# A transformer stack in fp32 pairs: the finished layer norm as operand from the seventh chunk of two feed-forwards on

## The reference

```python
x = layer_norm(ALPHA * x + y, ln_mix_g[layer], ln_mix_b[layer])
x = layer_norm(ALPHA * x + swiglu(x, ffn_w_gate[layer], ffn_w_up[layer], ffn_w_down[layer]),
               ln_ffn_g[layer], ln_ffn_b[layer])

def layer_norm(x, g, b):
    xf = x.astype(jnp.float32)
    mu = xf.mean(-1, keepdims=True)
    var = jnp.mean(jnp.square(xf - mu), -1, keepdims=True)
    return ((xf - mu) * lax.rsqrt(var + LN_EPS) * g.astype(jnp.float32) + b.astype(jnp.float32)).astype(x.dtype)

def swiglu(x, w_gate, w_up, w_down):
    return (jax.nn.silu(x @ w_gate) * (x @ w_up)) @ w_down
```

## Time and profile before

| | |
|---|---|
| median of three runs | 894.04 us (893.62 to 894.8) |
| the profiled execution | 892.68 us |
| its span | 890.9 us |
| TensorE busy | 881.3 us, 99% of the span |
| VectorE, ScalarE, GpSimd busy | 671.4, 511.8, 131.2 us |
| DMA | 156.82 MB |

### The profile page before, as it was taken

How to read it: one execution, slowest core, us unless ns; L and a number is a source line. 1 busy time by engine, 2 the same in 40 slices (tenths; PEclk the granted TensorE clock), 3 DMA queues, 4 the chain that set the end, 5 groups by cost and what they waited for, 6 DMA issues and landing times.

```text
span 890.9 us, 18060 instructions
## 1 busy us (share of the span) xinstructions
PE 881.3 (99%) x6704; PEld 831.8 (93%) x6704; DVE 671.4 (75%) x1114; ACT 511.8 (57%) x763; POOL 131.2 (15%) x89
## 2 busy tenths in 40 slices
PE   9999999999999999999999999999999999999997
PEld 8977999999999999999999999999899999999996
DVE  6976887777777966889766676789877886667666
ACT  7265644434344755977555655567488756555552
POOL 1000000000000043002232240210130122324003
PEclk9999999999999999999999999999999999999999
DMA  8963275555555554435655545434334465565541
GB/s 319 353 223 100 103 246 175 180 205 172 189 191 165 185 189 171 142 120 187 210 176 182 188 169 201 148 133 153 119 119 143 152 226 187 169 198 176 188 142 48
DMA packets 44291, 156.82 MB, mean 176 GB/s; under 512 B 5098, under 2 KB 5589, under 8 KB 44117
## 3 DMA queue, kind: packets, MB, share of 16 engines
q1 hardware_dynamic: 42889, 152.32, 50.2%
q10 hardware_dynamic: 908, 2.28, 0.8%
q0 software_dynamic: 448, 1.59, 0.5%
HBM read 155.11 MB, written 1.06 MB: 175 GB/s over the span
## 4 chain that ended last, share of the span: by engine, by line
PE 89%; DVE 6%; ACT 2%; DMA 1%; issue 1%; POOL 0%; DVEq 0%; POOLq 0%; SPq 0%
PE ps L434 21%; PE ps L435 20%; PE ps L436 20%; PE ps L506 5%; PE ps L508 5%; PE ps L507 5%; DVE w_lo L1476 2%; DMA raw<-in_stream 1%; PE ps L442 1%; PE ps L483 1%; PE ps L477 1%; PE ps L476 1%; PE ps L917 1%; PE ps L620 1%; PE ps L728 1%
## 5 line engine op out<-in xcount | busy, mean ns | idle before, releaser
L434 PE MATMUL ps<-op_hi,w_hi 128*128 128x258 f32 (+1 forms) x1306 | 370.1, 283 | 0.4 <-DVE op_lo L1663 0.4
L435 PE MATMUL ps<-op_lo,w_hi 128*128 128x258 f32 (+1 forms) x1306 | 368.1, 282 | 0.0
L436 PE MATMUL ps<-op_hi,w_lo 128*128 128x258 f32 (+1 forms) x1306 | 367.8, 282 | 0.0
L1476 DVE TENSOR_TENSOR w_lo<-raw,w_hi 128x1024 fp32r<-128x1024 f32 x222 | 283.1, 1301 | 24.7 <-ACT w_hi L1090 22.2
L1090 ACT ACTIVATE w_hi<-raw 128x1024 fp32r<-128x1024 f32 x223 | 230.4, 1052 | 68.8 <-PE ps L436 30.7
L434 PEld LDWEIGHTS ps<-op_hi,w_hi 128*128 128x128 f32 x1306 | 246.2, 188 | 3.8 <-issue 1.8
L435 PEld LDWEIGHTS ps<-op_lo,w_hi 128*128 128x128 f32 x1306 | 246.7, 189 | 1.7
L436 PEld LDWEIGHTS ps<-op_hi,w_lo 128*128 128x128 f32 x1306 | 246.3, 189 | 0.0
L1083 ACT ACTIVATE w_hi<-raw 128x1024 fp32r<-128x1024 f32 x60 | 63.5, 1058 | 60.0 <-PE ps L436 30.2
L434 PE MATMUL ps<-mix_hi,w_hi 128*128 128x256 f32 x336 | 95.6, 284 | 0.0
L436 PE MATMUL ps<-mix_hi,w_lo 128*128 128x256 f32 x336 | 94.1, 280 | 0.0
(11 more groups left out here) (313 smaller groups left out, 1113.8 us busy)
## 6 DMA issues: line engine op xcount, KB each, us to landing
raw<-in_stream SPq DMA_DIRECT2D x283, 512.0 KB, 3.7
bias<-bias_rows POOLq DMA_DIRECT2D x1, 1024.0 KB, 10.8
work<-in_last_norm SPq DMA_DIRECT2D x1, 1024.0 KB, 5.7
result<-y SPq DMA_DIRECT2D x4, 256.0 KB, 2.0
x<-in_x SPq DMA_DIRECT2D x3, 256.0 KB, 5.4
y<-in_spans ACTq DMA_DIRECT2D x1, 640.0 KB
raw<-in_stream SPq DMA_DIRECT2D x2, 256.0 KB, 3.4
bias<-bias_rows POOLq DMA_DIRECT2D x1, 512.0 KB, 13.5
```

The lines of the kernel that those rows point to most:

```text
L434: pe.matmul(o, wh, xh, start=start, stop=False, **kw)
L435: pe.matmul(o, wh, xl, start=False, stop=False, **kw)
L436: return pe.matmul(o, wl, xh, start=False, stop=stop, **kw)
L1476: m = dve.tensor_tensor(w_lo[:, s, :], raw[:, s, :], fp(w_hi[:, s, :]), ALU.subtract)
```

## The change

In the second and third feed-forward the operand of the up units changes at the seventh chunk (chunk 6). From there on it is the finished layer norm as a pair, with 256 columns: chunks 0 to 5 of it in `mix` chunks 2 to 7, chunks 6 and 7 in `p_both` (`normed`). TensorE waits for it on each turn of its loop.

- TensorE: two more chunks are written out (4 and 5, with the old operand); the loop has 7 turns. `up_normed` takes the place of `up` in the loop and in the last two chunks.
- VectorE: four multiplies of y by rinv (`scaled_pair`, behind chunks 1 to 4) that GpSimd made before, and four lo halves of the finished norm (`normed_lo_pair`, behind chunks 2 to 5). From chunk 6 on it no longer multiplies gate and up by rinv and no longer copies the shift column; it multiplies Silu and up result directly.
- ScalarE: four activations behind the Silu of each of the chunks 2 to 5 (`normed_pair`: hi half and fp32 x of two feature chunks). From chunk 6 on its Silu reads PSUM and waits for the gate unit.
- GpSimd: `normed_x` is gone; it only waits for `x_normed` and sums. It tells ScalarE by `alpha_made` when the scaled gain and shift are there, and ScalarE waits for that ahead of the third feed-forward.
- The first feed-forward computes as before.

```diff
-        mix_hi = sb("mix_hi", [P, NCH, SEQ], F32R)
-        mix_lo = sb("mix_lo", [P, NCH, SEQ], F32R)
-        p_hi = sb("p_hi", [P, 2, SEQ], F32R)
-        p_lo = sb("p_lo", [P, 2, SEQ], F32R)
+        mix = sb("mix", [P, 2, NCH, SEQ], F32R)
+        mix_hi, mix_lo = mix[:, 0], mix[:, 1]
+        p_both = sb("p_both", [P, 2, 2, SEQ], F32R)
+        p_hi, p_lo = p_both[:, 0], p_both[:, 1]
...
+        def normed(c, n=1):
+
+            both = mix[:, :, 2 + c:2 + c + n, :] if c < 6 else p_both[:, :, c - 6:c - 6 + n, :]
+            return both if n > 1 else both[:, :, 0, :]
...
-            def normed_x(gain, shift, scaled, j):
-
-                pool.wait_ge(S["rinv_copied"], scaled)
-                for i in range(4):
-                    chunk_passed(j + 2 + i)
-                    own.done(pool.tensor_tensor(pair(sq, i), pair(y, i), over(rinv[:, 0:SEQ], 2), ALU.mult))
-                own.settle()
-                for c in range(NCH):
-                    chunk_passed(j + 6 + c)
-                    pool.tensor_scalar(x[:, c, :], sq[:, c, :], gain[:, c:c + 1], shift[:, c:c + 1], ALU.mult, ALU.add
-                                       ).then_inc(S["x_normed"], 1)
+            def sum_normed_x(j):
+
...
-            normed_x(vcol("ln_mix_g", 0, 8), vcol("ln_mix_b", 0, 8), 2, NFF)
+            sum_normed_x(NFF)
...
             own.done(pool.tensor_scalar(alpha_gain[:], vcol("ln_mix_g", 8, 8), ALPHA, None, ALU.mult))
-            chained(pool.tensor_scalar(alpha_shift[:], vcol("ln_mix_b", 8, 8), ALPHA, None, ALU.mult))
-            normed_x(alpha_gain, alpha_shift, 4, 2 * NFF)
+            own.settle()
+            pool.tensor_scalar(alpha_shift[:], vcol("ln_mix_b", 8, 8), ALPHA, None, ALU.mult).then_inc(S["alpha_made"], 1)
+            sum_normed_x(2 * NFF)
...
+                def up_normed(c):
+                    for b in (4 + 2 * c, 5 + 2 * c):
+                        s = take()
+                        for k in range(NCH):
+                            w, x_both = slice(k * P, k * P + P), normed(k)
+                            m = three(bank(b, 0, SEQ), w_hi[:, s, w], w_lo[:, s, w], x_both[:, 0, :], x_both[:, 1, :],
+                                      k == 0, k == NCH - 1)
+                        given(m)
...
-                turns = NFF // 2 - 3
+                later = up
+                if shifted:
+                    down(0, j + 3)
+                    up(0)
+                    down(1, j + 4)
+                    up(1)
+                    norms[0] += 1
+                    later = up_normed
+                done = 2 if shifted else 0
+                turns = (NFF - done) // 2 - 3
                 with pe.Fori(0, turns) as i:
                     unit.enter(i, 6)
-                    down(0, i * 2 + (j + 3))
-                    up(0)
-                    down(1, i * 2 + (j + 4))
-                    up(1)
+                    down(0, i * 2 + (j + 3 + done))
+                    if shifted:
+                        pe.wait_ge(S["normed_hi"], NCH * norms[0])
+                        pe.wait_ge(S["normed_lo"], 4 * norms[0])
+                    later(0)
+                    down(1, i * 2 + (j + 4 + done))
+                    later(1)
...
+            def normed_pair(i, gain, shift, own_gain, own_shift):
+
+                act.wait_ge(S["to_norm"], 4 * normed_n[0] + i + 1)
+                for c in (2 * i, 2 * i + 1):
+                    act.activation(normed(c)[:, 0, :], sq[:, c, :], ACT.Identity, bias=shift[:, c:c + 1],
+                                   scale=gain[:, c:c + 1]).then_inc(S["normed_hi"], 1)
+                    act.activation(x[:, c, :], sq[:, c, :], ACT.Identity, bias=own_shift[:, c:c + 1],
+                                   scale=own_gain[:, c:c + 1]).then_inc(S["x_normed"], 1)
...
+                    if whole:
+                        act.wait_ge(S["units_done"], unit.at(-1))
+                    else:
+                        act.wait_ge(S["conv_done"], j + (convs[0] + 1))
...
+                        m = act.activation(gate[:, c, :], bank(4 + 2 * c, 0, SEQ), ACT.Silu)
...
+                    if norm and isinstance(j, int) and 2 <= j < 6:
+                        normed_pair(j - 2, *norm)
...
             normed_operand("ln_mix_g", "ln_mix_b", 1)
-            feed_forward(False, late=2, mean=4)
+            act.wait_ge(S["alpha_made"], 1)
+            feed_forward(False, late=2, mean=4,
+                         norm=(vcol("ln_mix_g", 8, 8), vcol("ln_mix_b", 8, 8), alpha_gain, alpha_shift))
...
+            def scaled_pair(i):
+
+                dve.tensor_tensor(pair(sq, i), pair(y, i), over(rinv[:, 0:SEQ], 2), ALU.mult).then_inc(S["to_norm"], 1)
+
+            def normed_lo_pair(i, scaled_by):
+
+                dve.wait_ge(S["x_normed"], (NCH * 2 if scaled_by else 0) + 2 * i + 2)
+                dve.wait_ge(S["normed_hi"], NCH * normed_n[0] + 2 * i + 2)
+                both = normed(2 * i, 2)
+                if scaled_by:
+                    m = dve.scalar_tensor_tensor(both[:, 1], pair(x, i), 1.0 / scaled_by, fp(both[:, 0]),
+                                                 ALU.mult, ALU.subtract)
+                else:
+                    m = dve.tensor_tensor(both[:, 1], pair(x, i), fp(both[:, 0]), ALU.subtract)
+                m.then_inc(S["normed_lo"], 1)
...
-                        if part == 0:
+                        if part == 0 and not whole:
...
+                    elif whole:
+                        dve.wait_ge(S["gate_act"], j + (j0 + 1))
+                        chained(dve.tensor_tensor(h_fp[:, c, :], gate[:, c, :], chunk(up + 1, 0), ALU.mult))
...
+                for j in range(1, 4 if convolve else 6):
+                    if j > 1:
+                        step()
+                    hidden_chunk(j % 2, j)
+                    if not convolve and j < 5:
+                        scaled_pair(j - 1)
+                    if not convolve and j > 1:
+                        normed_lo_pair(j - 2, scaled_by)
```

More of the change, by code:

```diff
@@ L1237, in hidden_chunk @@
                     m.then_inc(S["gate_act"], 1)
+                    if norm and isinstance(j, int) and 2 <= j < 6:
+                        normed_pair(j - 2, *norm)
                 hidden_chunk(0, 0)
                 hidden_chunk(1, 1)
-                step()
-                hidden_chunk(0, 2)
-                step()
-                hidden_chunk(1, 3)
-                turns = NFF // 2 - 3
+                for j in range(2, 4 if convolve else 6):
+                    step()
+                    hidden_chunk(j % 2, j)
+                done = 0 if convolve else 2
+                turns = (NFF - done) // 2 - 3
+                if norm:
+                    normed_n[0] += 1
                 per = sum(centred(split.n + i) for i in range(6))
@@ L1251, in feed_forward @@
                     step()
-                    hidden_chunk(0, i * 2 + 4)
+                    hidden_chunk(0, i * 2 + (4 + done), whole=not convolve)
                     step()
-                    hidden_chunk(1, i * 2 + 5)
+                    hidden_chunk(1, i * 2 + (5 + done), whole=not convolve)
                     unit.leave(turns)
@@ L1258, in feed_forward @@
                 step()
-                hidden_chunk(0, NFF - 2)
+                hidden_chunk(0, NFF - 2, whole=not convolve)
                 if mean:
@@ L1262, in feed_forward @@
                 step()
-                hidden_chunk(1, NFF - 1)
+                hidden_chunk(1, NFF - 1, whole=not convolve)
                 step(ahead=not late)
@@ L1266, in feed_forward @@
                 hidden.n = j0 + NFF
+                convs[0] += NFF if convolve else 6
+            convs = [0]
             act.wait_ge(S["pool_const"], 1)
@@ L1341, in _ @@
             normed_operand("ln_mix_g", "ln_mix_b", 0)
-            feed_forward(False, mean=2)
+            layer_gain, layer_shift = vcol("ln_mix_g", 0, 8), vcol("ln_mix_b", 0, 8)
+            feed_forward(False, mean=2, norm=(layer_gain, layer_shift, layer_gain, layer_shift))
             normed_operand("ln_ffn_g", "ln_ffn_b", 0)
@@ L1815, in feed_forward @@
                 hidden_chunk(0, 0)
-                hidden_chunk(1, 1)
-                step()
-                hidden_chunk(0, 2)
-                step()
-                hidden_chunk(1, 3)
-                turns, per = NFF // 2 - 3, 8 + 2 * convolve
+                for j in range(1, 4 if convolve else 6):
+                    if j > 1:
+                        step()
+                    hidden_chunk(j % 2, j)
+                    if not convolve and j < 5:
+                        scaled_pair(j - 1)
+                    if not convolve and j > 1:
+                        normed_lo_pair(j - 2, scaled_by)
+                done = 0 if convolve else 2
+                if not convolve:
+                    normed_n[0] += 1
+                turns, per = (NFF - done) // 2 - 3, 10 if convolve else 4
                 with dve.Fori(0, turns) as i:
@@ L2131, in _ @@
```

(2 more changed lines are left out.)

17 lines of the change are left out of this document (10 added, 7 removed).

## The result

| | before | changed kernel |
|---|---|---|
| median of nine runs each | 893.99 us (892.77 to 894.8) | 896.1 us (895.09 to 898.28) |
| ratio of the two | | 1.0025, 95% interval 1.0016 to 1.0034 |
| the profiled execution, its span | 892.68, 890.9 us | 896.34, 894.5 us |

The account below looks back on a forecast made before the run. TensorE, busy 881.3 of 890.9 us, was taken as the bound. Up matmuls -4.15, third-entry stall +2.60 and seventh chunk +0.05 gave -1.5 us, 894.04 to 892.5 us; range 890.0 to 895.6.

Parts of the forecast that it names:

- so I take 117.3: Up matmuls from the seventh chunk: 117.3 ns each instead of 120.0, read from the gate products behind the first block.
- The stall at the third entry: Third feed-forward: ScalarE waits for alpha_made, so TensorE stalls 2.6 us before its first down unit; bounds 2.3 to 3.6.
- rival B: No stall at the third feed-forward's entry because the wait is hidden: 889.9 us; chance 6%.
- rival C: Granted clock falls from 2.4 to 1.2 GHz behind the third entry's stall; 8 us there gives 896.5 us; chance 8%.
- it decides for slower once more than 6.6 us are spent there: Low clock behind the third entry's stall: each us costs 0.5, so over 6.6 us there makes the kernel slower.
- My row against it: End of the span: TensorE idle 4.2 us after the last matmul with the clock still at 1.00, cited against rival C.
- The up matmuls: Second and third feed-forward, from the seventh chunk: 1536 matmuls 2.7 ns shorter each, 4.15 us less; lower end 1.84.
- rival A: Only the column count matters, so up matmuls on the new tile run at 118.8 ns: 894.8 us; chance 20%.
- the down units, in the loop, run at 117.1 on mix: Down matmuls of 256 columns in the second feed-forward's loop: 117.1 ns, cited against rival A.
- The seventh chunk: TensorE waits there for all four lo halves: 0.05 us for the two places, up to 0.5 each if VectorE is late.
- Rival D: Late lo halves: TensorE waits 0.5 to 2 us at the seventh chunk of both feed-forwards; 893.5 to 896.5 us; chance 4%.
- The new work of VectorE and ScalarE in chunks 1 to 5: Chunks 1 to 5: added multiplies, lo halves and activations hidden under TensorE, costed at nothing.

Follow-up runs that it names:

- e9: The changed kernel run again unaltered, its third trace: 894.36 us, one run.
- e1: The changed kernel with GpSimd's alpha_gain and alpha_shift moved ahead of its last two roots: 891.05 us against 893.6, ratio 0.9969.
- e10: e1 run again unaltered, its second trace: 891.46 us, one run.
- e11: e1 with the rows of the op tiles 272 elements apart instead of 258, the same kernel as e7: 887.33 us, ratio 0.9929.
- e5: e1 with ScalarE made to wait, ahead of the third feed-forward, for GpSimd's root of the norm: 895.59 us, one run.
- e6: e1 with ScalarE made to wait, ahead of the third feed-forward, for VectorE's variance: 894.54 us, one run.
- e3: e1 with the second feed-forward loop's down matmuls in the third's 512-column form (part of that product in the wrong layout): 892.32 us, one run.
- e12: The kernel before, run again unaltered, its second trace: 896.96 us, one run.
- e8: The changed kernel run again unaltered, its second trace: 896.13 us, one run.
- e7: e1 with the op tiles' rows 272 elements apart instead of 258: ratio 0.9923; five ordinary runs 886.09 to 888.16 us, the sixth 2205.67.

## Why the prediction was wrong, step by step

Two steps of the sum failed, of nearly the same size. The clock behind the stall was put at nothing and cost 1.2 to 1.5 us. And "so I take 117.3" for the up matmuls held in the third feed-forward, but in the second only in one of three traces; in the other two it gave back 1.3 to 1.5 us. A third, smaller one is the down matmuls, left as they were: 0.4 us.

*The stall at the third entry (+2.60).* Right in every link: ScalarE idle 4.4 us with GpSimd as releaser (4.39), alpha_shift 0.24 without VectorE beside it (0.23), the table load as the last thing ahead of the Silu, 2.6 us in front of the first down unit (2.61). No reading was missing here; rival B falls.

*The clock behind it (rival C, 8%).* The step that failed is "it decides for slower once more than 6.6 us are spent there", together with its chance. I asked only whether the clock alone could turn the forecast over, and took no part of it into the sum. It fell in all three traces of the changed kernel, for some 3 us, at 1.2 to 1.5 us each time. The timed runs fit that: none of the nine has a mean granted clock above 0.998, while 25 of the 31 of the kernel before that were taken beside the experiments have 0.999 or 1.0. My row against it was misread, because its window ended too soon. The next one of the same trace, with TensorE still idle:

```profile
889.50:890.80 1.30, 0.00 (x0) 0.50 0.37 145
```

So the clock did fall there, 4.3 us behind the last matmul. The row showed a clock that holds for a while and then falls; it could not be held against a fall.

*The up matmuls (-4.15).* As a size of the lower level this was right: 117.34 ns measured, 1536 x 2.69 = -4.13. But two things around it failed. First, "the tile of rows 4, so I take 117.3" took one draw of a two-level quantity for a property of the form. At the upper level, in the second feed-forward, the change gives back 1.3 to 1.5 us, and it did so in two of three traces. This is not rival A: its 118.8 came from counting columns, and e9 has 117.34 with the same columns and the same program. Second, "the down units, in the loop, run at 117.1 on mix" was used as evidence, and their own time left as it was. They changed beside the new up units: 15 units of 12 in the third feed-forward by 2.0 ns each, 0.36 us, and in the second 117.15 to 117.34, 0.07 over some 360. With these, -4.13 + 0.43 = -3.70; e1 and e10, which have nothing else in the way, show -3.51 and -3.64.

*The seventh chunk (+0.05).* Right. Timelines of VectorE and TensorE in the changed kernel:

```profile
447.54 0.69 DVE L1817 TENSOR_TENSOR p_both<-x,p_both 128x512 fp32r<-128x512 f32 x1
...
448.50 0.35 PE L431 MATMUL ps<-mix,w_hi 128*128 128x256 f32 x1
448.69 0.28 PE L432 MATMUL ps<-mix,w_hi 128*128 128x256 f32 x1
```

The last lo half ends at 448.23. The first matmul behind the wait for it is 0.07 us longer than its neighbours (0.35 against 0.28), and the next starts 0.19 behind it in place of 0.12; in the third feed-forward, from 748.68, it is 0.21. So some 0.16 us for both, against 0.05. Rival D falls. The new work of VectorE and ScalarE in chunks 1 to 5 and the shorter loop cost nothing, as forecast, and VectorE's split became faster without GpSimd beside it, to no use: 1270 ns in the mean against 1301.

*The sum.* Over the two stretches the forecast was -1.5. The traces give +1.9, +2.0 and +0.5: -3.6 (matmuls), +2.70 (idle), +1.2 to +1.5 (clock), and in the first two +1.3 to +1.5 (upper level). No one of the missing terms makes the kernel slower by itself; clock and down matmuls together bring it from -1.5 to +0.3 or more (e9: +0.5), the upper level to +1.9. The medians differ by 2.1. Whether the nine timed runs mostly stood at the upper level was not traced, but for the first of them; e9, at the lower, took 894.36 us, less than any of the nine (895.09 at least).

## What to carry to other kernels

Price a stall of the bounding engine with what comes behind it: here 1.4 us of idle time cost 1.4, 2.7 us cost 4.0 to 4.2, because the matmuls behind it ran at half the clock. Take it as a risk and not as a limit: halts of 2.0 to 2.35 us brought the fall in some traces and not in others. And when a row is to speak against a rival, read on until the state ends. When a small instruction gets a new waiter, move it ahead of the long work in its engine's program; here two instructions of 0.24 us, moved ahead of two roots, were worth 4 us. A spacing that the argument rests on should be read in more than one execution, and a small difference counted between two points inside the program, since the part ahead of the second feed-forward alone scattered by 4 us.

## What the runs showed of the hardware that I had not expected

- In two stages (the gate products behind the first block, the second feed-forward's loop) back-to-back matmuls of one form settle at one of two spacings for the whole stage, 117.3 or 118.7 ns for 256 columns at a granted clock of 1.00, and the same program shows both. In the third feed-forward only 117.3 came, in nine traces.
- The spacing depends on more than the instruction's own operands: the row step of the op tiles, 258 or 272 elements, moved the up matmuls from 120.03 to 119.42 ns, down matmuls on another tile from 117.15 to 116.74, and in e11 a loop that doesn't read those tiles from 117.34 to 116.67. Whether it is the step or the address at which the other tiles come to lie was not told apart. The Trainium skill ("TensorE: Matmul & The Clock Gate", Back-to-back issue gap) has a formula for an isolated gap in which only the columns count, and says that a real stream of weight loads and matmuls is set by both. These runs show 118.66 and 117.34 ns for the same 256 columns, and 120.03 and 119.42 for the same 258.
- At the third entry the granted clock fell from 2.4 to 1.2 GHz with 2.20 us (e5) and 2.70 us (changed kernel, three traces) between two matmuls, and with 1.42 us (e6) it did not. Near 57 us it fell behind 2.09, 2.19 and 2.25 us (e6, e3, e12) and held behind 2.03, 2.14, 2.26 and 2.35 us (e8, e11, e5, e10). In the changed kernel seven matmuls ran at the low clock, from 710.26 to 713.31.
- One execution of e7 took 2205.67 us and is left out above: its loop matmuls stood 298 ns apart, while VectorE's busy time was 641.8 us as ever. Its trace holds no record of the granted clock, so the clock isn't ruled out. No run explains it.
